# Constant products in TensorE's waits, and a part of the shared expert ahead of the routing wait

## The reference

```python
for l in range(DEPTH):
    h = rmsnorm(x, norm1_g[l]) * (1 + mod[:, 1]) + mod[:, 0]       # and the same for the context
    y, yc = mix_tokens(h, hc, ...)       # one projection, then attention (3 kinds) and a chunked delta-rule scan
    x = x + mod[:, 2] * y
    h = rmsnorm(x, norm2_g[l]) * (1 + mod[:, 4]) + mod[:, 3]
    f = moe_ffn(h, ...)
    x = x + mod[:, 5] * f
return rmsnorm(x, final_norm_g)

def moe_ffn(x2, w_router, bias, w_gate, w_up, w_down, sw_gate, sw_up, sw_down):
    scores = sigmoid(x2 @ w_router)      # 64 experts; groups of 8 chosen first, then 6 experts per token
    ...
    shared = (silu(x2 @ sw_gate) * (x2 @ sw_up)) @ sw_down
    return routed + shared
```

## Time and profile before

| what | value |
|---|---|
| timed runs | 2292.69, 2305.5, 2319.4 us, median 2305.5 us |
| span of the profiled execution | 2310.2 us, 4.7 us above that median |
| PE busy | 2022.2 us, 88% |
| DVE / ACT / GpSimd (POOL) busy | 687.0 / 488.6 / 272.1 us |
| HBM read | 556.26 MB |

### The profile page before, as it was taken

How to read it: one execution, slowest core, us unless ns; L and a number is a source line. 1 busy time by engine, 2 the same in 40 slices (tenths; PEclk the granted TensorE clock), 3 DMA queues, 4 the chain that set the end, 5 groups by cost and what they waited for, 6 DMA issues and landing times.

```text
span 2310.2 us, 33886 instructions
## 1 busy us (share of the span) xinstructions
PE 2022.2 (88%) x13908; PEld 1169.1 (51%) x13908; DVE 687.0 (30%) x1563; ACT 488.6 (21%) x1113; POOL 272.1 (12%) x316
## 2 busy tenths in 40 slices
PE   6989998979888999999996897999868888888884
PEld 3445567974533444444443665689753333333333
DVE  2022277551561111111112442666252111111113
ACT  2102265431201111111111212634211111111111
POOL 0030001210101111111110000022011111111110
PEclk8999999999889999999997999989979999999997
DMA  9586410001089999999995411100149999999983
GB/s 388 193 227 223 154 37 2 4 3 59 37 324 389 421 418 404 389 377 388 393 371 242 193 36 37 37 3 4 60 188 397 416 390 392 403 405 401 398 337 131
DMA packets 136121, 558.57 MB, mean 242 GB/s; under 512 B 27424, under 2 KB 60925, under 8 KB 85917
## 3 DMA queue, kind: packets, MB, share of 16 engines
q1 hardware_dynamic: 109757, 494.74, 53.2%
q0 software_dynamic: 24192, 38.54, 4.9%
q10 hardware_dynamic: 2016, 23.07, 2.4%
HBM read 556.26 MB, written 46.14 MB: 261 GB/s over the span
## 4 chain that ended last, share of the span: by engine, by line
PE 57%; DMA 29%; DVE 7%; SPq 2%; ACT 2%; issue 2%; POOL 0%; ACTq 0%; POOLq 0%; DVEq 0%
PE bank L786 52%; DMA ring<-in_moe_w_up 14%; DMA arena<-in_moe_w_up 11%; PE bank L789 5%; DMA ring<-in_w_ada 1%; DMA ring<-y_rows 1%; DVE arena L1312 1%; SPq L579 1%; ACT arena L2004 1%; DVE h_t L1312 1%; ACT L2004 1%; SPq L567 1%; DVE h_t L1315 1%; DVE ring L1312 0%; DVE arena L1338 0%
## 5 line engine op out<-in xcount | busy, mean ns | idle before, releaser
L786 PE MATMUL bank<-ring,arena 128*64 128x512 f32 (+4 forms) x2688 | 722.4, 522 | 70.5 <-DMA ring<-in_moe_w_up 53.0
L786 PE MATMUL bank<-arena 64*64 64x64 f32 (+6 forms) x5676 | 700.2, 323 | 50.0 <-DMA ring<-in_moe_w_up 20.1
L786 PEld LDWEIGHTS bank<-arena 64*64 64x64 f32 (+3 forms) x5676 | 354.7, 148 | 261.2 <-issue 239.1
L786 PEld LDWEIGHTS bank<-ring,arena 128*64 128x64 f32 (+3 forms) x2688 | 273.0, 152 | 346.5 <-issue 336.8
L2001 ACT ACTIVATE arena<-bank 128x256 f32<-128x256 f32 (+5 forms) x472 | 211.8, 459 | 584.5 <-PE bank L786 396.9
L1312 DVE TENSOR_TENSOR arena<-arena,bank 128x256 f32<-128x256 f32 (+2 forms) x112 | 47.6, 425 | 711.6 <-ACT arena L2004 691.3
L789 PEld LDWEIGHTS bank<-cst,arena 128*128 128x128 f32 (+2 forms) x1214 | 163.9, 181 | 162.7 <-issue 121.3
L789 PE MATMUL bank<-cst,arena 128*128 128x128 f32 (+2 forms) x1214 | 194.9, 300 | 36.2 <-DVE arena L1315 9.8
L786 PE MATMUL bank<-ring,h_t 128*128 128x384 f32 (+5 forms) x800 | 212.3, 427 | 9.2 <-ACT h_t L2004 9.2
L2004 ACT ACTIVATE arena<-bank 128x256 f32<-128x256 f32 (+2 forms) x90 | 33.6, 378 | 713.2 <-PE bank L786 713.2
L2443 POOL DMA_INDIRECT y_rows<-h_t,arena x80 | 79.9, 999 | 877.1 <-DVE h_t L1927 877.1
(11 more groups left out here) (184 smaller groups left out, 1259.8 us busy)
## 6 DMA issues: line engine op xcount, KB each, us to landing
ring<-in_moe_w_gate SPq DMA_DIRECT2D x78, 1024.0 KB, 14.5
ring<-in_moe_w_up SPq DMA_DIRECT2D x78, 1024.0 KB, 23.3
ring<-in_moe_w_down SPq DMA_DIRECT2D x78, 1024.0 KB, 19.7
arena<-in_moe_w_gate SPq DMA_DIRECT2D x50, 1024.0 KB, 14.9
arena<-in_moe_w_up SPq DMA_DIRECT2D x50, 1024.0 KB, 23.8
arena<-in_moe_w_down SPq DMA_DIRECT2D x50, 1024.0 KB, 18.0
ring<-in_w_ada SPq DMA_DIRECT2D x52, 576.0 KB, 5.4
ring<-in_w_in SPq DMA_DIRECT2D x12, 1152.0 KB, 12.3
```

The costliest lines, as they stand in the source:

```text
L786: return pe.matmul(o, a, b, start=first, stop=last)
```

## The change

A new helper `stay_busy(b, n)` issues `n` products of the identity with 512 columns of the constants tile `cst` into a bank `b` whose content nothing reads before it is written again. It stands at ten places ahead of a wait, nine of them inside the loop over layers (111 products in all: 50 in layer 0, 54 in layer 1, 7 at the end). In layer 1 the first place issues its 4 products ahead of the input projection. Two places get an extra wait ahead of the products, for the copy that empties the bank. In addition `shared_up` can be cut into ranges of its 8 products: in layer 0 the first 3 products of the third pass, in layer 1 all 8, are moved ahead of the wait for `rt.vc`, behind a wait for `rt.sig` that stood further down.

```diff
+            def stay_busy(b, n):
+                for _ in range(n):
+                    mm(bank[b][:], ident, cst[:, 0:512])
...
                     turn_modulation(2)
+                stay_busy(5 if l == 0 else 0, 3 if l == 0 else 4)
...
                     if k == 7:
+                        stay_busy(3, 4 if l == 0 else 6)
                         wait('DVE', 'lat.norm', l, NT - 1, 0)
...
                     if k == 0:
+                        wait('ACT', 'up.out', l, 0)
+                        stay_busy(6, 2)
                         wait('DVE', 'rope.q.sum', l)
...
+                stay_busy(0, 2)
                 wait('DVE', 'att.y', l, tiles(l) - 1, 1)
...
                     if (s, name) == (0, 'kk'):
+                        wait('ACT', 'gq.out', l, 2)
+                        stay_busy(3, 2)
                         wait('ACT', 'gq.out', l, 6)
...
+                stay_busy(scan_bank(l, 3, 0, 'sn0'), 9 if l == 0 else 7)
                 wait('DVE', 'gdn.end', l)
...
                 squares_sum(l, 'norm2', n_tok)
+                stay_busy(2, 6 if l == 0 else 3)
                 pe.wait_ge(*loaded(l, 'router'))
...
-                def shared_up(f, g):
+                def shared_up(f, g, k0=0, k1=KD):
-                    for k in range(KD):
+                    for k in range(k0, k1):
...
                 shared_up(0, 1)
+                wait('ACT', 'rt.sig', l)
+                early = 3 if l == 0 else KD
+                shared_up(1, 0, 0, early)
                 wait('DVE', 'rt.vc', l)
...
                 wait('DVE', 'rt.mask', l)
-                wait('ACT', 'rt.sig', l)
...
-                shared_up(1, 0)
+                if early < KD:
+                    shared_up(1, 0, early)
                 wait('DVE', 'rt.perm', l)
...
                 wait('DVE', 'rt.flag', l)
+                stay_busy(0, 2 if l == 0 else 8)
...
+                stay_busy(0, 20)
                 wait('Pool', 'xg.diag', l)
...
+            stay_busy(4, 7)
             wait('DVE', 'fin.scale', 0, KD - 1)
```

More of the change, by code:

```diff
@@ L1118, in _ @@
                 wait('DVE', 'out.x', l, KD - 1, 0)
-                def shared_up(f, g):
-                    for k in range(KD):
+                def shared_up(f, g, k0=0, k1=KD):
+                    for k in range(k0, k1):
                         last = mm(bank[4 + 2 * f + g][:, 0:n_tok], gu[:, g, k, P * f:P * f + P], hT[:, k, 0:n_tok], k == 0, k == KD - 1)
-                    last.then_inc(*done('PE', 'sh.up', l, f, g))
+                    if k1 == KD:
+                        last.then_inc(*done('PE', 'sh.up', l, f, g))
                 def shared_down(m):
```

## The result

The changed kernel took 2279.1 us (median of four runs, 2274.3 to 2280.0), the kernel before beside it 2306.3 us (four runs, 2292.69 to 2319.4). The ratio is 0.9871, with a 95% interval of 0.9834 to 0.9908: 1.3% less time. The forecast was 2280.0 us, with a range of 2263 to 2298.

What follows compares the result with a forecast made beforehand. PE was taken to bound the kernel, except where expert weights are awaited, with some 300 us at half clock. Terms summed to 25.2 us saved, 8.8 from moved products and 16.4 from the clock, giving 2280.0 us, range 2263 to 2298.

Steps and rivals of the forecast that it cites:

- lat.norm: Ahead of the normed latents' transposes: 10 products shorten the half-speed stretch behind, +6.4 us in both layers (bounds 0 and 8.7).
- rope.q.sum: Ahead of rope.q.sum: no wait to fill, 4 products cost 3.6 us, half given back; -1.8 us (bounds -3.6 and 0).
- att.y: Ahead of att.y: products overhang 1.0 us of waits but may lift the clock for the transposes; +0.4 us (-6 to +4).
- kk: Ahead of the scan's kk: products delay DVE and the scan behind it; -1.6 us for both layers (bounds -3.6 and 0).
- gdn.end: Ahead of the head output's transposes: 16 products in 16.8 us of waits save half-speed work behind; +3.0 us (-1 to 3.4).
- router: Ahead of the router: 9 products let it start at full speed, perhaps not stay there; +3.2 us with layer 1.
- moved products: Around the routing transposes: ids copied 4.4 us sooner per layer, so the experts' stage starts earlier; +8.8 us (5 to 10).
- rt.flag: Behind rt.flag: 10 products, 8 in a wait for gathered rows; 0 to 3.7 us per layer, +3.0 together.
- The clock is given back: Rival: half-clock stretches return a little later, some 40% of clock gains remain; about 2297 us, chance 0.32.
- Transposes lose the clock: Rival: the clock falls in transposes behind lat.norm, gdn.end and the last wait; 2288 us, chance 0.05.
- The experts' stage swallows what comes before it: Rival: weight flow doesn't move with the ids, savings ahead of it are lost; 2302 us, chance 0.07.
- The fill is the new wait: Rival: products run at half clock, 1.78 us each, and overhang the waits by 95 us; about 2390 us, chance 0.03.

Runs made afterwards that it cites:

- with the ids first: Changed kernel without products ahead of rope.q.sum and kk, layer 0's five remaining third-pass products put behind the ids product; 2283.1 us, 0.9857 of the kernel before.
- kernel with four places: Changed kernel with constant products only ahead of lat.norm, gdn.end, the router and fin.scale, moved products kept; 2279.1 us, 0.9857 of the kernel before.

## Why the prediction was right, and where its sum was not

The time came out as forecast, 0.9 us off, but not because each term was right. That it is so close is luck: the router brought 8.3 us more than forecast and the experts' stage 4.6 less, and the runs of one kernel scatter by more than the 0.9. The mechanism, half-clock stretches behind waits that filling the waits takes away, and ids that come sooner, is what the runs show. Term by term:

| term | forecast | shown | by |
|---|---|---|---|
| projections | +0.7, +1.4 | +1.4, +1.7 | sum of squares to the end of the 8 products, 26.02 to 24.58; the long piece of layer 1, 79.55 to 77.88 |
| lat.norm, both layers | +6.4 | +6.1 | 24.50 to 21.35 and 24.31 to 21.33 us from the transposes to the second scores, without rope's products |
| rope.q.sum | -1.8 | -1.2 | 0.6 in each layer |
| att.y | +0.4 | open | see below |
| kk | -1.6 | -1.8 | two times 1.5, less 1.2 |
| gdn.end | +3.0 | +3.1 | leads up to the router, +1.7 and +1.4 |
| router | +3.2 | +11.5 | the kernel without its products |
| moved products | +8.8 | +9.1 | leads, +4.3 and +4.8; alone 4.3 and 4.7 |
| rt.flag and the experts | +3.0 | -1.6 | leads from ids to adding up, -0.2 and -1.4 |
| adding up and end | +1.7 | +1.6 and more | lead at the end; adding up in layer 0 is mixed with the projection behind it |

*The step that failed most* is the router's: "the clock did not rise while it worked on the 64-column products", from which the text took "they start at full speed but need not stay there". The first is right: without the products it is 13.88 us at half once more. The second does not follow from it. PE arrived at full clock, and 7.33 us of the same products, then the transposes, ran at 1.00 all through [after, 587.03 to 599.40]. Work that doesn't lift the clock can still keep it: so it was in layer 0 of all eleven profiles with products there. Yet it need not. In layer 1 three of the eleven lost the clock inside the router, though PE came to it at full clock (the kernels with the constant products alone, with the ids first and without att.y's products); it then took 4.57 to 4.65 us. Layer 1's router in the changed kernel, then in the one with the constant products alone:

```profile
1654.97 3.76 PE L786 MATMUL bank<-ring,h_t 128*128 128x64 f32 x32 [0.93 <-ACT h_t L2025]
```

```profile
1664.28 4.65 PE L786 MATMUL bank<-ring,h_t 128*128 128x64 f32 x32 [0.93 <-ACT h_t L2022]
```

```profile
1664.28:1668.93 4.65, 4.65 (x34) 0.78 0.01 4
```

So the forecast's doubt had a ground, but its price is 0.9 us and not most of the gain. What decides between the two is open. The bounds, 0 and 9.1 in layer 0, did hold the 7.6.

*The other one* is rt.flag. In layer 1 the lead did rise behind it, from 32.1 us at the ids to 35.2 at the second unit (1742.62 before, 1707.44 after), but at the adding-up it was 30.8. In layer 0 nothing came at all; the half-clock stretch at 651.25 stayed. The kernel with four places, which has no products behind rt.flag, loses 1.7 and 0.9 us from ids to adding up, 2.6 together; the changed kernel's two profiles have 1.6 and 3.0. The forecast counted what PE saves at the stage's door; its own remark that an earlier PE helps "only as far as it frees a slot sooner" was the better guide.

*The moved products* had the right size, and a reason that holds only in part. The text said that the experts' loads start earlier and so "the stage starts earlier as a whole". The loads do start earlier, but the kernel with the ids ahead of everything shows that PE's own list decides: there the loads come another 2.0 us sooner and the stage ends later. The gain is the waiting that PE no longer does ahead of rt.vc (2.52 to 0.21 us in layer 0, 3.79 to 0.38 in layer 1), and the half-clock stretch behind that wait, which goes with it.

*Places without a wait.* rope.q.sum and kk cost, as forecast, and the reasons given (GpSimd's wait behind one, DVE behind the other) show in the rows. For att.y the products ran at half clock in both layers of the changed kernel. From the last 96-wide transposes to kk, kk's products not counted, layer 1 took 66 and 68 us without them (two profiles) and 69 to 74 with them (nine), but the half-clock stretch there begins ahead of the products, and the kernel before has 72 as well. Whether they cost anything there is open.

The terms shown add up to 29.9 us, of a lead of 32.4 in that profile; the rest lies in attention, the scan and the start.

*Rivals.* "The clock is given back" is wrong for the changed kernel: no half-clock stretch came back behind lat.norm, gdn.end, the router and the end. It is right in small for the experts' stage, and for layer 1's router in three other kernels. "Transposes lose the clock" is refuted by the kernel that fills with transposes alone; the rule of the Trainium skill (TensorE: Matmul & The Clock Gate, Part 4: PE-mode transpose) does not hold in these runs. "The experts' stage swallows what comes before it" is refuted by the leads. "The fill is the new wait" did not happen. Doubling the counts made a wait of it, though not at half clock, as the rival had it.

## What to carry to other kernels

A wait of PE costs twice: its own length, and, if the clock falls, half of what PE works in the half-clock stretch behind it. The second part can be bought back with work that nothing reads, up to the end of the wait and not beyond. It paid most ahead of the router, whose 64-column products began at half and stayed there for 13.88 us, or began at full and mostly stayed there too. Put it where the trace shows a wait ending late and a half-speed stretch behind it (here four of ten places did nearly all of it), and leave out steps that only name a wait. Read gains as leads between two traces at the same instruction, place by place: the sum can be right by luck.

## What was not expected of the hardware

The level depends on what came before, not only on the work itself: the same 64 records took 13.88 us (arriving at half, behind 5.72 us of waiting) and 7.33 us (arriving at full).

The start of the kernel is not steady. Eight profiles (the changed kernel twice, the one without rope.q.sum and kk twice, those without the router's, kk's and att.y's products, and the one with the ids first) have one and the same instruction list of PE up to lat.norm, and reach its transposes between 270.54 and 276.81 us, 6.3 us apart. In that part PE waits for pieces of `w_ada` and the clock falls behind such a wait, or falls for a shorter time. The window 142.75 to 153.00 has a mean granted clock of 0.50 in the changed kernel and 0.83 in the second profile without rope.q.sum and kk, PE being busy for 8.8 and 8.9 us of it. That is a part of the scatter of some 10 us between runs of one kernel. A difference of a few microseconds between two spans means nothing; the same difference inside one stretch can be read.
